# Activations of the dense stages at other remainders modulo 256 than the weights

## What is computed

```
h = rmsnorm(x, norm1_g)
z = h @ w_in                                  # 1024 -> 3328 + 1536 + 2048
y_a = rwkv7_time_mix(z_rwkv, ...) @ w_proj_a
y_b = window_sink_attention(q, k, v, sink) @ w_proj_b
x = x + (g_a * y_a + g_b * y_b) @ w_out
x = x + conv_ffn(rmsnorm(x, norm2_g), w_up, conv_w, conv_b, w_down)   # 1024 -> 2 x 2816 -> 1024
return rmsnorm(x, normf_g)
```

## Time and profile before

| | |
|---|---|
| median of two runs | 1065.61 us (1065.18 to 1066.04) |
| the profiled execution | 1065.44 us, of which its span is 1063.8 us |
| TensorE busy | 1047.4 us, 98% of the span, 6746 matmuls |
| DVE, ACT, POOL busy | 674.2, 499.5, 130.5 us |
| TensorE clock granted | 0.999 of 2.4 GHz |

### The profile page before, as it was taken

The page is one execution under the profiler, slowest core; times in us unless marked ns, Lnnn a source line. Parts: engine busy times, 40 slices in busy tenths (PEclk is TensorE's granted clock), DMA queues, the critical chain, the costliest instruction groups (busy, mean ns, idle before and its releaser), DMA issues.

```text
span 1063.8 us, 17993 instructions
## 1 busy us (share of the span) xinstructions
PE 1047.4 (98%) x6746; PEld 839.6 (79%) x6746; DVE 674.2 (63%) x1158; ACT 499.5 (47%) x859; POOL 130.5 (12%) x195
## 2 busy tenths in 40 slices
PE   7999999999999999999999999999999999999997
PEld 6887888777777777777777888888888888888886
DVE  4224656587988878878776445457777777752234
ACT  6436675633534445335444333565565556531122
POOL 8100000220220321313210110100000000000000
PEclk9999999999999999999999999999999999999999
DMA  7632322321212313314242554423333333323321
GB/s 205 156 92 88 92 88 80 100 63 41 63 35 60 95 49 83 81 50 118 75 144 88 151 158 119 139 80 99 99 92 104 89 99 91 99 99 99 99 80 79
DMA packets 156087, 101.48 MB, mean 95 GB/s; under 512 B 31369, under 2 KB 144311, under 8 KB 156023
## 3 DMA queue, kind: packets, MB, share of 16 engines
q1 hardware_dynamic: 148800, 79.72, 25.6%
q0 software_dynamic: 7072, 20.83, 7.4%
q10 hardware_dynamic: 151, 0.04, 0.0%
HBM read 91.65 MB, written 8.91 MB: 95 GB/s over the span
## 4 chain that ended last, share of the span: by engine, by line
PE 94%; DVE 3%; ACT 1%; issue 1%; DMA 1%; SPq 0%; DVEq 0%; ACTq 0%
PE ps L1748 16%; PE ps L1751 16%; PE ps L1750 16%; PE ps L1704 5%; PE ps L1706 4%; PE ps L1705 4%; PE ps L2252 4%; PE ps L2251 4%; PE ps L2253 4%; PE ps L1886 3%; PE ps L2013 2%; PE ps L2034 2%; PE ps L1830 1%; PE ps L1966 1%; PE ps L1943 1%; PE ps L1923 1%
## 5 line engine op out<-in xcount | busy, mean ns | idle before, releaser
L1164 DVE TENSOR_TENSOR wlo<-raw,whi 128x1024 fp32r<-128x1024 f32 x128 | 156.7, 1224 | 207.0 <-ACT whi L763 137.3
L763 ACT ACTIVATE whi<-raw 128x1024 fp32r<-128x1024 f32 x124 | 131.0, 1057 | 111.7 <-PE ps L1751 108.6
L1748 PE MATMUL ps<-xnh,whi 128*128 128x512 f32 x344 | 133.9, 389 | 0.0
L1751 PE MATMUL ps<-xnh,wlo 128*128 128x512 f32 x344 | 133.8, 389 | 0.0
L1750 PE MATMUL ps<-xnl,whi 128*128 128x512 f32 x344 | 133.8, 389 | 0.0
L1748 PE MATMUL ps<-xh,whi 128*128 128x512 f32 x248 | 98.6, 398 | 1.2 <-DVE xl L1182 1.2
L1750 PE MATMUL ps<-xl,whi 128*128 128x512 f32 x248 | 96.8, 390 | 0.0
L1751 PE MATMUL ps<-xh,wlo 128*128 128x512 f32 x248 | 96.6, 389 | 0.0
L1704 PE MATMUL ps<-xh,whi 128*128 128x512 f32 x184 | 85.2, 463 | 0.4 <-DVE wlo L1164 0.4
L1750 PEld LDWEIGHTS ps<-xnl,whi 128*128 128x128 f32 x344 | 64.6, 188 | 13.5
L1748 PEld LDWEIGHTS ps<-xnh,whi 128*128 128x128 f32 x344 | 64.6, 188 | 13.4
(11 more groups left out here) (358 smaller groups left out, 2203.0 us busy)
## 6 DMA issues: line engine op xcount, KB each, us to landing
raw<-in_w_in SPq DMA_DIRECT2D x108, 256.0 KB, 3.0
raw<-in_w_up SPq DMA_DIRECT2D x88, 256.0 KB, 3.0
raw<-in_w_down SPq DMA_DIRECT2D x44, 256.0 KB, 2.8
gates_scratch<-gst POOLq DMA_DIRECT2D x16, 256.0 KB, 3.4
raw<-in_w_proj_b SPq DMA_DIRECT2D x16, 256.0 KB, 3.9
raw<-in_w_proj_a SPq DMA_DIRECT2D x16, 256.0 KB, 3.0
gl<-gates_scratch POOLq DMA_DIRECT2D x16, 256.0 KB, 3.0
raw<-in_w_out SPq DMA_DIRECT2D x16, 256.0 KB, 2.9
```

Of the source, the lines that this page charges most:

```text
L763: act.activation(flat(whi[:, hb]), flat(raw[:, b]), ACT.Copy).then_inc(w_hi, 1)
L1164: dve.tensor_tensor(flat(lo[:, hb]), flat(raw[:, b]), flat(hi[:, hb]).bitcast(F32), ALU.subtract).then_inc(w_lo, 1)
L1748: pe.matmul(ps[bank][:, :], whi[:, hb, k, :], hi(k), start=first and k == 0, stop=False)
L1751: ins = pe.matmul(ps[bank][:, :], wlo[:, hb, k, :], hi(k), start=False, stop=last and k == kn - 1)
```

## The change

Only byte offsets change. `ZR` moves by 256 bytes, and `QR`, `KVR` and all that hangs on them with it, which keeps their remainders modulo 256. The dense activations get an addition of their own:

| stage | activations | stationary | moving | remainder of the activations, before | after |
|---|---|---|---|---|---|
| input projection, filler too | xh, xl | weights | xh, xl | 0 | 64 |
| projection of the time mix | yah, yal | weights | yah, yal | 0 | 32 |
| projection of the attention | ybh, ybl | weights | ybh, ybl | 0 | 0 |
| output projection | mh, ml | weights | mh, ml | 0 | 0 |
| up projection | xnh, xnl | weights | xnh, xnl | 0 | 192 |
| down projection | hh, hl | hh, hl | weights | 0 | 32 |

`raw`, `whi`, `wlo`, `whx`, `wlx` and the result tile `yt` stay where they are. No instruction is added, removed or reordered on any engine, and no wait changes: in the built programs the two differ in addresses alone.

```
-        XHL, ZR, QR, KVR = 0, 32 * K, 80 * K, 96 * K
+        XHL = 0
+        ZR = XHL + 32 * K + 256
+        QR, KVR = ZR + 48 * K, ZR + 64 * K
...
-        xh = at(XHL, "xh", [P, KT, T], F32R)
-        xl = at(XHL + 16 * K, "xl", [P, KT, T], F32R)
+        xh = at(XHL + 64, "xh", [P, KT, T], F32R)
+        xl = at(XHL + 64 + 16 * K, "xl", [P, KT, T], F32R)
...
-        yah = at(XHL, "yah", [P, KT, T], F32R)
-        yal = at(XHL + 16 * K, "yal", [P, KT, T], F32R)
+        yah = at(XHL + 32, "yah", [P, KT, T], F32R)
+        yal = at(XHL + 32 + 16 * K, "yal", [P, KT, T], F32R)
...
-        hh = at(ZR, "hh", [P, FT, T], F32R)
-        hl = at(ZR + 2 * K * FT, "hl", [P, FT, T], F32R)
-        X1 = ZR + 4 * K * FT
+        hh = at(ZR + 32, "hh", [P, FT, T], F32R)
+        hl = at(ZR + 32 + 2 * K * FT, "hl", [P, FT, T], F32R)
+        X1 = ZR + 4 * K * FT + 256
...
-        xnh = at(XHL, "xnh", [P, KT, T], F32R)
-        xnl = at(XHL + 16 * K, "xnl", [P, KT, T], F32R)
+        xnh = at(XHL + 192, "xnh", [P, KT, T], F32R)
+        xnl = at(XHL + 192 + 16 * K, "xnl", [P, KT, T], F32R)
```

## The result

The changed kernel takes **1078.49 us** (median of two runs, 1078.41 to 1078.56) against 1065.61 us before: a ratio of 1.0121, with a 95% interval from 1.0103 to 1.0138. It is slower, by 12.9 us, where I forecast no change. The time lies inside the range and within 2%, and where the slower rival put it (1079).

What follows compares the result with a forecast made beforehand. TensorE's time for its matmuls was taken to bound the kernel. 1065.4 us of the profiled execution plus 0 for every term gave 1065 us, with an 8-in-10 range from 1040 to 1084 us.

Steps and rivals of the forecast that it cites:

- the slower rival: Moved dense matmuls: equal remainders were the good case; 231 ns steps give 1079 us, 238.7 give 1102; chance 0.27.
- What bounds the kernel: Whole kernel: TensorE, busy 98% of the span, sets the time; a dense matmul's step is 226.7 ns.
- The 3.07 us for each nanosecond: All 3072 matmuls that read a moved activation: each nanosecond of their step is worth 3.07 us.
- (1): Queues: no instruction, wait or DMA is added or moved, so no term.
- (2): Regions from ZR on shift by 256 bytes and keep their remainders: costed at nothing.
- (3): ACT and DVE writes of activations at new remainders: nothing within 10 ns, under 1 us in all and hidden.
- (4): The 3072 matmuls reading a moved activation: step changes by 0 ns, bounded by 13.4 ns less and 12 ns more.
- the upper bound: Dense matmul with an f16 load under it: 0.24 us step, 12 ns more, 37 us in all.
- The sign for it: Attention's projection and output projection, still at remainder 0, should keep 226.7 ns in any case.
- the unsettled 231 ns of the earlier trace: Eight steps right after transposes average 231 ns on the same tiles and remainders, so the excess isn't constant.
- The faster rival: Moved dense matmuls: equal remainders collide, moving them apart removes excess; all gives 1024 us, half 1044; chance 0.31.
- the lower bound: Moved dense matmuls: nothing can go under the columns themselves, 13.4 ns less, 41 us in all.

Runs made afterwards that it cites:

- per256: The changed kernel with all four additions (xh, yah, xnh, hh) at 256 bytes: 1065.78 us.
- sub1: The kernel before with xh and xl at remainder 16, xnh and xnl at 8, hh and hl at 16, all else at 0: 1078.99 us.
- sub3: The kernel before with xh and xl at remainder 252, xnh and xnl at 12, hh and hl at 188, all else at 0: 1072.30 us.
- sub5: The kernel before with the activations of the input projection at remainder 160, up projection at 48, down projection at 204: 1082.78 us.
- map2: The changed kernel with other additions: input projection 32, time mix's projection 160, up projection 64, down projection 192: 1073.99 us.
- map1: The changed kernel with other additions: input projection 128, time mix's projection 96, up projection 32, down projection 64: 1080.86 us.
- all192: The kernel before with weights and arena moved together to remainder 192, so their difference stays 0: 1065.65 us.
- experiment 6: The changed kernel with only one half of each activation pair moved, by 64 or by 192: 1077.58 and 1074.00 us; also the changed kernel's attention tiles.
- wlo64: The kernel before with only the low weights wlo 64 bytes further, whi and all activations still at remainder 0: 1076.75 us.

## Why the prediction was wrong, step by step

**What bounds the kernel: right.** TensorE's steps are the time; 6.7 ns more on the 1032 and 528 matmuls between the starts compared are 6.9 and 3.5 us, and the traces show 6.8 and 3.5. The 3.07 us for each nanosecond was only roughly right: it takes every moved matmul for one with a settled step. At the same difference of 64 the undisturbed part of the input projection lost 2.2 ns a step, the input projection as a whole 1.3 us by 1296 matmuls, 1.0 ns each.

**(1), (2), (3), no other cost: right.** `per256` clears the shift of the regions. The writes at 32 cost nothing: the answer to the earlier trace rows for `hl` is 693 ns for 692.

**(4), "by these rows I take 0 ns": the step that failed.** The change of the step is not 0: it is 6.7 ns in the up and the down projection, 6.8 in the time mix's and 2.2 in the undisturbed part of the input projection, 13.2 us of span in all, 4.3 ns by the mean of the 3072 matmuls. I had one comparison that varied the remainder, `n1` against `xx` in the earlier trace rows (differences 96 and 0), and took it to speak for the dense loads. The trace after answers it with both pairs now at other differences (160 and 64):

```profile
401.60 0.40 PE L1708 MATMUL ps<-xh,wlo 128*128 128x512 f32 x1
401.84 0.41 PE L1945 MATMUL ps<-yy,n 128*128 128x64 f16 x8
...
402.64 0.40 PE L1708 MATMUL ps<-xh,wlo 128*128 128x512 f32 x1
402.88 0.41 PE L1968 MATMUL ps<-v,xx 128*128 128x64 f16 x8
```

Still 0.24 us each. In 13 of the 16 kernels the median of the steps before `n` and before `xx` is 237 to 239 ns, about 12 above the dense 226.7, at a difference of 0 as at others; only `sub1` (`xh` at 16: 230 before `n`, 240 before `xx`), `sub3` and `sub5` (232 to 234) have others. So the row could not show how the dense step behaves. (The 12 ns of the upper bound fit this median; from the rounded 0.24 us of the rows alone it would be 13 ns, 41 us.)

A row that reacts was in the trace: the f32 transposes of `sc`, loaded at remainder 0 under a matmul on `xh`. I had not used it, and before the change it has only one difference. Across the kernels it moves. Under `map2` (difference 32), then under `map1` (128):

```profile
114.67 0.40 PE L1753 MATMUL ps<-xh,wlo 128*128 128x512 f32 x1
114.91 0.82 PE L2115 MATMUL ps<-ident,sc 128*128 128x128 f32 x6
```

```profile
114.53 0.39 PE L1753 MATMUL ps<-xh,wlo 128*128 128x512 f32 x1
114.76 0.93 PE L2115 MATMUL ps<-ident,sc 128*128 128x128 f32 x7
```

237 ns in all seven places of `map2`, 229 or 230 in all seven of `map1`, 232 or 233 before. That shows that there is a dependence, not what it does to the dense step: here difference 0 is dearer than 128, there it is the cheapest.

The earlier trace rows misled in another way, which I had only called weaker: the steps between the f32 transposes of `z` and of `bp` are 107 to 110 ns for 128 columns, half the pace of a dense matmul, in every kernel, also in `all192`, where both tiles move by 192 against `ident`. They do not react. That the slower pace is the reason is not shown.

**The rivals.** The slower one came true. That its number fits so well is in part luck: I had put 231 ns in every moved stage and 1079 us; the up and the down projection took 233.3, more than that, and the input projection lost 1.0 ns a matmul instead of 4.6, and the two errors largely cancel. The sign for it, that unmoved stages keep 226.7, held for the output projection's total (50.1 us); the attention's tiles behind one of the time mix took 228.2 by the mean, from the eight steps behind each tile of the time mix (experiment 6). Its evidence, the unsettled 231 ns of the earlier trace rows, was the right row: a step that varies on the same tiles has something that can come out of step. I weighed it below two rows that held still. The faster rival, a collision at equal remainders, is refuted: 0 is the cheapest of 20 differences tried. The upper bound from the f16 row, 238.7 ns, held: the worst point of the map is 237.9. So did the lower bound, with nothing near it.

**The Trainium skill's rule** (SBUF — State Buffer, "Who interferes with whom") says that the two read ports of TensorE are independent and PE never waits on anyone. I had read it as saying that remainders can't matter. For `fp32r` the runs do not agree with that: the same instructions take from 226.7 to 237.9 ns by where the two operands lie, and in `wlo64` the place of the loaded weights alone changed the matmuls' step. Whether the two ports are what interferes, no run shows. I had given that rule no term in the sum, but it stood behind the same answer.

**The range** held the time, and 0.27 for the slower rival was too little for what the earlier trace rows showed.

## What to carry to other kernels

Where dense `fp32r` matmuls with a weight load each bound the time, place both operands at the same remainder modulo 256, halves of a split included, and look at the step (start to start), not at the busy time or the durations. A buffer moved by a few bytes cost this kernel up to 2% with not one instruction changed, so an edit of layout needs the step before and after. To judge from a trace whether something matters, take the comparison from the same type and pace of instruction. And where matmuls are often interrupted by others, expect less than the settled price.

## What the runs showed of the hardware

- The settled step of a 512-column `fp32r` matmul with a load under it is 226.7 ns at 2.4 GHz when all operands lie at the same remainder modulo 256, and 228.9 to 237.9 ns at the 19 other differences tried. Four bytes are the worst case found, 12 and 64 the mildest (228.9).
- Shifting both operands together (by 192 bytes), or one by 256, changes nothing.
- The steps settle into repeating cycles, 232, 226 and 229 ns at a difference of 64 for example, and the mean of a cycle isn't the mean of its pairs' prices. Behind a tile at difference 32, matmuls at difference 0 take eight steps of 231 ns on the mean before they are at 227 again. Why, and why 240 settles at 236.7 ns in one stage and 233.3 in another, stays open; so does what part of the 13.4 ns above the columns at difference 0 is due to the load, since no run here has a dense matmul without one.
